# Decay sums of a gated linear attention with high and low parts of 64 tokens stacked on the contraction rows

## The reference

```python
def gla_chunked(q, k, v, log_a):
    """S_t = diag(a_t) S_{t-1} + k_t v_t^T, o_t = q_t S_t."""
    ...
    bc = jnp.cumsum(ac, axis=3)
    ...
        o_inter = jnp.einsum('bhtk,bhkv->bhtv', qi * jnp.exp(bi), state)
        diff = bi[:, :, :, None, :] - bi[:, :, None, :, :]
        decay = jnp.exp(jnp.where(causal[:, :, None], diff, -jnp.inf))
        scores = jnp.einsum('bhtk,bhsk,bhtsk->bhts', qi, ki, decay)
```

## Time and profile before

| | |
|---|---|
| time of the runs shown | 903.37, 903.11, 903.11 us; median 903.11 |
| span of the profiled execution, first to last instruction | 901.3 us |
| PE busy | 893.6 us, 99% of the span |
| DVE busy | 624.8 us, 69% |
| ACT busy | 504.8 us, 56% |
| POOL busy | 79.0 us, 9% |
| granted TensorE clock, mean | 0.999 |

### The profile page before, as it was taken

How to read it: one execution, slowest core, us unless ns; L and a number is a source line. 1 busy time by engine, 2 the same in 40 slices (tenths; PEclk the granted TensorE clock), 3 DMA queues, 4 the chain that set the end, 5 groups by cost and what they waited for, 6 DMA issues and landing times.

```text
span 901.3 us, 12594 instructions
## 1 busy us (share of the span) xinstructions
PE 893.6 (99%) x4946; PEld 761.6 (85%) x4946; DVE 624.8 (69%) x793; ACT 504.8 (56%) x701; POOL 79.0 (9%) x145
## 2 busy tenths in 40 slices
PE   9999999999999999999999999999999999999998
PEld 7888878887889888888889988777888888888887
DVE  5646566765876566666585898998887595666664
ACT  6646655545355444444466878977464564444441
POOL 8603342130010000000000000000000000000000
PEclk9999999999999999999999999999999999999999
DMA  8654333466554655555545764443446376556551
GB/s 274 222 187 152 128 102 121 152 225 220 184 157 156 218 187 186 186 186 187 187 141 186 236 189 139 134 131 112 139 147 209 111 233 191 185 190 201 182 170 47
DMA packets 103380, 155.27 MB, mean 172 GB/s; under 512 B 2650, under 2 KB 70338, under 8 KB 103331
## 3 DMA queue, kind: packets, MB, share of 16 engines
q1 hardware_dynamic: 102416, 151.57, 51.6%
q0 software_dynamic: 864, 2.98, 1.0%
q10 hardware_dynamic: 50, 0.04, 0.0%
HBM read 153.53 MB, written 1.05 MB: 172 GB/s over the span
## 4 chain that ended last, share of the span: by engine, by line
PE 96%; ACT 1%; issue 1%; POOL 0%; DMA 0%; DVE 0%; POOLq 0%; ACTq 0%; DVEq 0%
PE PS L628 19%; PE PS L630 19%; PE PS L629 19%; PE PS L1017 15%; PE PS L1022 8%; PE PS L681 3%; PE PS L687 1%; PE PS L907 1%; PE PS L1153 1%; PE PS L1131 1%; PE PS L1065 1%; PE PS L1189 1%; PE PS L894 0%; PE PS L858 0%; DMA res<-in_x_dram 0%
## 5 line engine op out<-in xcount | busy, mean ns | idle before, releaser
L1937 DVE TENSOR_TENSOR wlo<-raw,whi 128x2048 fp32r<-128x2048 f32 x141 | 324.2, 2301 | 124.0 <-ACT whi L1341 122.3
L1341 ACT CAST whi<-raw 128x2048 fp32r<-128x2048 f32 x141 | 269.2, 1909 | 112.1 <-PE PS L630 109.2
L1017 PE MATMUL PS<-hT,whi 128*128 128x512 f32 x608 | 144.7, 390 | 0.0
L1017 PEld LDWEIGHTS PS<-hT,whi 128*128 128x128 f32 x608 | 113.2, 188 | 23.2 <-issue 0.2
L628 PE MATMUL PS<-whi,hT 128*128 128x512 f32 (+1 forms) x320 | 126.2, 395 | 0.0
L630 PE MATMUL PS<-whi,hT 128*128 128x512 f32 (+1 forms) x320 | 123.1, 385 | 0.0
L629 PE MATMUL PS<-wlo,hT 128*128 128x512 f32 (+1 forms) x320 | 122.9, 384 | 0.0
L628 PE MATMUL PS<-whi,aT_hi 128*128 128x512 f32 x216 | 84.3, 391 | 0.0
L629 PE MATMUL PS<-wlo,aT_hi 128*128 128x512 f32 x216 | 84.3, 390 | 0.0
L630 PE MATMUL PS<-whi,aT_lo 128*128 128x512 f32 x216 | 84.0, 389 | 0.0
L1022 PEld LDWEIGHTS PS<-hT,wlo 128*128 128x128 f32 x608 | 78.0, 191 | 3.0
(11 more groups left out here) (385 smaller groups left out, 1303.5 us busy)
## 6 DMA issues: line engine op xcount, KB each, us to landing
raw<-in_w_in_dram SPq DMA_DIRECT2D x47, 1024.0 KB, 5.1
raw<-in_w_ff_dram SPq DMA_DIRECT2D x32, 1024.0 KB, 5.5
raw<-in_w_gate_dram SPq DMA_DIRECT2D x11, 1024.0 KB, 5.3
raw<-in_w_up_dram SPq DMA_DIRECT2D x11, 1024.0 KB, 5.3
raw<-in_w_down_dram SPq DMA_DIRECT2D x11, 1024.0 KB, 5.0
raw<-in_w_out_dram SPq DMA_DIRECT2D x8, 1024.0 KB, 5.0
raw<-in_w_proj_gla_dram SPq DMA_DIRECT2D x4, 1024.0 KB, 6.6
raw<-in_w_mem_kv_dram SPq DMA_DIRECT2D x4, 1024.0 KB, 5.0
```

The lines of the kernel that those rows point to most:

```text
L1017: pe.matmul(PS[:, bank + c, :], w_hi[:, k, c * P:(c + 1) * P], hT[:, k, :, :].rearrange("p w t -> p (w t)"), start=k == 0, stop=False, ski ...
L1341: act.copy(whi[:, n % RING, :], raw[:, n % RING, :]).then_inc(hi_made, 1)
L1937: dve.tensor_tensor(wlo[:, n % RING, :], raw[:, n % RING, :], whi[:, n % RING, :].bitcast(F32), ALU.subtract).then_inc(lo_made, 1)
```

## The change

The sums are made of 64 tokens at a time. The 128 rows of the contraction hold the rounded part of 64 tokens and their rest together, so that one matmul adds both. For each unit four matmuls of 256 columns (four levels by 64 tokens) stand in place of four of 512. The matrix `decay_r` is folded: its rows repeat after 64. Sums that reach over the middle of the 128 tokens, which are those of the first and the last block only, are no longer complete; `gla_carry` multiplies the half that lacks it by the factor of the other half (`whole`, one column of `E`). The gate's parts are written in halves of 64 partitions, where DVE's rest goes to the partitions that the rounded part leaves. POOL's constants get eight instructions in place of the rounded copy.

```diff
-        a_hi = [w[:, 10:12, :].rearrange("p f t -> p (f t)") for w in (oT_hi, oT_lo)]
-        a_lo = [aT_lo[:, a, :, :].rearrange("p b t -> p (b t)") for a in range(TT)]
+        a_parts = [[oT_hi[:, 10:12, :].rearrange("p f t -> p (f t)"), oT_lo[:, 10:12, :].rearrange("p f t -> p (f t)")],
+                   [aT_lo[:, i, :, :].rearrange("p b t -> p (b t)") for i in range(2)]]
+        HALF = [slice(0, 64), slice(64, 128)]
...
         def gla_carry(engine, u):
 
             h, a = u // 2, u % 2
-            tok = slice(a * P, a * P + P)
-            if a == 0:
-                return engine.tensor_tensor(K7, E[:, 0, :], gkT[:, h, tok], ALU.mult)
-            return engine.tensor_tensor(Q7, E[:, 7, :], gqT[:, h, tok], ALU.mult)
+            x, src, of = (HALF[0], E[:, 0, :], K7) if a == 0 else (HALF[1], E[:, 7, :], Q7)
+            whole = E[:, 7, P - 1:P] if a == 0 else E[:, 7, 63:64]
+            y = HALF[1 - a]
+            other = (gkT if a == 0 else gqT)[:, h, a * P:a * P + P]
+            if u in SHARED_UNITS:
+                engine.tensor_tensor(of[:, y], src[:, y], other[:, y], ALU.mult)
+                return engine.scalar_tensor_tensor(of[:, x], src[:, x], whole, other[:, x], ALU.mult, ALU.mult)
+            engine.tensor_scalar(of[:, x], src[:, x], whole, None, ALU.mult).then_inc(carry, 1)
+            engine.tensor_tensor(of[:, y], src[:, y], other[:, y], ALU.mult)
+            engine.wait_ge(carry, CARRIES.index(u) + 1)
+            return engine.tensor_tensor(of[:, x], of[:, x], other[:, x], ALU.mult)
...
-            step(pool.tensor_copy(decay_r, decay_sum))
+            first, second = decay_sum[:, :, 0:64], decay_sum[:, :, 64:128]
+            for s in range(2):
+                step(pool.tensor_tensor(decay_r[:, s, 0:1, :], first[:, 7:8, :], second[:, 0:1, :], ALU.add))
+                step(pool.tensor_tensor(decay_r[:, s, 1:7, :], first[:, 1:7, :], second[:, 1:7, :], ALU.add))
+                step(pool.tensor_tensor(decay_r[:, s, 8:9, :], first[:, 8:9, :], second[:, 7:8, :], ALU.add))
+                step(pool.tensor_copy(decay_r[:, s, 7:8, :], decay_r[:, s, 8 * s:8 * s + 1, :].bitcast(F32)))
...
                 for c in range(2):
-                    d = decay_r[:, a + 4 * c:a + 4 * c + 4, :]
-                    pe.matmul(PS[:, 6 + c, :], a_hi[a][:, h * P:(h + 1) * P], d, start=True, stop=False)
-                    mm = pe.matmul(PS[:, 6 + c, :], a_lo[a][:, h * P:(h + 1) * P], d, start=False, stop=True)
+                    for s in range(2):
+                        mm = pe.matmul(PS[:, 6 + c, :].rearrange("p (l t) -> p l t", t=P)[:, :, HALF[s]],
+                                       a_parts[a][s][:, h * P:(h + 1) * P], decay_r[:, s, a + 4 * c:a + 4 * c + 4, :],
+                                       start=True, stop=True)
...
                 act.wait_ge(ga_min, a + 1)
-                act.copy(a_hi[a], t).then_inc(ga_hi, 1)
+                for s in range(2):
+                    act.copy(a_parts[a][s][HALF[s], :], t[HALF[s], :]).then_inc(ga_hi, 1)
...
-                dve.wait_ge(ga_hi, a + 1)
-                dve.tensor_tensor(a_lo[a], t, a_hi[a].bitcast(F32), ALU.subtract).then_inc(ga_made, 1)
+                for s in range(2):
+                    dve.wait_ge(ga_hi, 2 * a + s + 1)
+                    dve.tensor_tensor(a_parts[a][s][HALF[1 - s], :], t[HALF[s], :], a_parts[a][s][HALF[s], :].bitcast(F32),
+                                      ALU.subtract).then_inc(ga_made, 1)
```

More of the change, by code:

```diff
@@ L145, in two_block_kernel @@
         SIG_EXP = [f"gout{c}" for c in range(4)] + ["cg0", "cg1"]
-        CONSTS = 1 + 1 + 4 * LEVELS + 1 + 1 + 3 + 1 + 3 * LEVELS + 1
+        CONSTS = 1 + 1 + 4 * LEVELS + 1 + 8 + 3 + 1 + 3 * LEVELS + 1
         PS = ctx.enter_context(nc.psum_tensor("PS", [P, 8, 512], F32))
@@ L216, in two_block_kernel @@
         decay_sum = TMP[:, 0:1152].rearrange("p (l t) -> p l t", t=P)
-        decay_r = aT_hi[:, :, :, :].rearrange("p r a t -> p (r a t)")[:, 0:1152].rearrange("p (l t) -> p l t", t=P)
+        decay_r = aT_hi[:, :, :, :].rearrange("p r a t -> p (r a t)")[:, 0:1152].rearrange("p (s l t) -> p s l t", s=2, t=64)
         mask = TMP[:, 1152:2176].rearrange("p (l t) -> p l t", t=P)
@@ L227, in two_block_kernel @@
         SHARED_UNITS, LOW_LEVELS = (0, 1, 5, 6, 7), 4
+        CARRIES = [u for u in range(2 * GLA_H) if u not in SHARED_UNITS]
         def gla_factor(engine, u, l):
@@ L317, in two_block_kernel @@
             sem(n) for n in ("ga_y", "ga_l", "ga_min", "ga_hi", "ga_made"))
+        carry = sem("carry")
         gf_sum, gf_exp, gf_qk, gf_up, gs_made, gs_masked, gs_ready, gs_x = (
@@ L843, in sb_scores @@
                     pe.wait_ge(drained[unit_of["sbk0"] % 2], unit_of["sbk0"] // 2 + 1)
-                    pe.wait_ge(ga_made, 2)
+                    pe.wait_ge(ga_made, 2 * TT)
                 for b in range(2):
```

## The result

The changed kernel takes 906.35 us (median of 6, 905.68 to 906.60) beside 903.24 us for the kernel before: a ratio of 1.0034, 95% interval 1.0024 to 1.0043. It is slower by 3.1 us, above the range of 900.5 to 904.5 us, and on the side of the rival with the clock. The profiled span is 903.9 us where it was 901.3.

A forecast was written before the change was run, and what follows sets the result against it. PE bounds the kernel, busy 893.6 of 901.3 us. Matmuls -3.05, unit 3 +2.43 and the gate +0.70 sum to +0.08 us, so 903.2 us; range 900.5 to 904.5 us.

The forecast's parts named there:

- the rival with the clock: After PE's 3.3 us wait in unit 3 the clock falls to 1.2 GHz; 905.2 us at 4 us; chance 0.08.
- the rule S/2: On PE behind unit 3's wait: S us at 1.2 GHz cost S/2; slower than 904.9 us from S = 3.6.
- The matmuls: In the sums, four matmuls of 256 columns for four of 512 save PE 0.435 us a unit; seven units 3.05 us.
- The rival of the weight load: The sums' new matmuls go at their weight load's pace, 191 ns, gaining 0.15 us a unit; 905.2 us; chance 0.05.
- Unit 3: POOL's third carry instruction waits behind DVE's split, PE starts the scores at 132.74 us; cost 2.43 us.
- DVE first: In unit 3 DVE's split starts at 130.22 us, 0.02 us ahead of POOL's third instruction.
- the first rival: In unit 3 POOL's third instruction starts ahead of DVE's split; unit 3 costs 0.31 us, total 901.1 us; chance 0.36.
- The gate: Two more ACT roundings ahead of emptying chunk n = 2 delay PE at chunk n = 4; cost 0.70 us.
- The share that I gave to POOL's constants: At the gate, a POOL sum of 64 columns holds DVE's split 0.32 us at most; 0.17 us taken.
- the rival of the lock at the gate: POOL's 384-column sum starts just ahead of DVE's split at 24.42, gate 1.0 us later; 904.2 us; chance 0.09.
- The other units: Unit 4's carry keeps 0.14 us of room, no cost; units 0, 1, 2, 5, 6 and 7 have more room.

The follow-up runs named there:

- e5: Changed kernel with ten unread 128x128 matmuls on PE ahead of unit 3's scores: 904.62 us, ratio 1.0019 to the kernel before.
- e1: Kernel before with only the sums' matmuls changed, four of 256 columns per unit, half the products left out: 899.91 us beside 903.03.
- e8: Changed kernel with unit 3 shared with DVE and the gate's second half moved behind chunk n = 4: 898.88 us, ratio 0.9953.
- e9: Kernel before with unit 3 shared with DVE and the gate's second half behind chunk n = 4: 902.37 us, ratio 0.9993.
- e4: Changed kernel with one added wait, so DVE starts its split only after POOL's carry of unit 3: 902.76 us, ratio 0.9993.
- e3: Kernel before with only POOL's carry of units 2, 3 and 4 in three instructions: 904.01 us, ratio 1.0012.
- e6: Changed kernel with unit 3 among the units shared between POOL and DVE: 900.21 us, ratio 0.9971 to the kernel before.
- e7: Changed kernel with the gate's second half moved behind chunk n = 4 on ACT and DVE: 905.20 us, ratio 1.0021.

## Why the prediction was wrong, point by point

**The step that failed** is the clock. The forecast had PE wait 3.3 us in unit 3 and kept the granted clock at 1.00 behind it, at no cost, since it had stayed there through a wait of 1.4 us. A wait of 1.4 us says nothing about one of 3.3. PE waited 3.55 us, the clock went to 1.2 GHz for some 3.4 us, and 1.62 us went there. e5 shows it: POOL as late as ever, the clock held, 1.7 us back. This was the slower rival, at a chance of 0.08, with the rule S/2 and, for S = 4, 905.2 us. The rule held (3.4/2 = 1.7 us); the chance did not, for no row had a wait of that length at a clock of 1.00. Of the 3.1 us between 903.2 forecast and 906.35 measured the clock is the largest term; the rest are the gate with 0.41, unit 3 with 0.18, unit 4 with 0.23, the later start with 0.14, and 0.5 us that stay open.

**The matmuls** were right: 0.44 us a unit, 3.1 us in e1, 3.5 us with all eight units in e8 against e9. The rival of the weight load (191 ns for each) is refuted by starts 0.12 us apart.

**Unit 3** was right in mechanism and nearly in size: 2.43 us forecast, 2.55 on the timeline, or 2.61 counted from chunk n = 15. Most of the difference is the split itself, 2.45 us in place of 2.29 behind POOL's second product. What I had by 0.02 us, DVE first, was 0.25 us in truth (130.18 and 130.43), because the scaling by a column takes 0.45 us and not 0.24. The select was the wrong row for it. That DVE came first was called rightly, but by luck: the sum's 0.02 us were smaller than its error of 0.2. With the right value the first rival (0.36) had almost no chance left. e4 (the race undone) and e3 (the race not lost) settle it.

**The gate** was right in mechanism and mis-sized: 0.70 us forecast, 1.25 - 0.14 = 1.11 us in the profile. The base of it, two more roundings, was 1.06 us with each at 0.53; they took 0.64 each, four of them 2.58 us where two had taken 1.05. ACT started line 1416 at 33.02 where line 1400 started at 31.33, 1.69 us later: 1.53 are these roundings, 0.15 a later start of the gate. DVE's emptying ends 1.70 us later, at 34.35, and PE starts 0.14 behind its end. Before, 0.59 us lay between that end and PE's start (33.24 less 31.96 and 0.69), so 0.45 of it was room: 1.70 - 0.45 = 1.25 us. The share that I gave to POOL's constants, 0.17, was small in the profiled execution (the split took 2.38 us, 0.09 more) and is 0.8 us in the profile of e6. The forecast placed a short sum ahead of the split; in three of the six profiles it was the one of 384 columns. So the rival of the lock at the gate (0.09) is real, and its chance was too low, though it doesn't explain the profiled execution.

**The other units** cost little: units 4 to 7 gave 1.51 us of 1.74. The 0.23 us that are missing arise at unit 4, where the forecast had 0.14 us of room left and no cost. The scaling's 0.21 us more use that up. POOL's third product ends at 150.40, PE's last matmul of the chunk starts at 150.09, and the scores, due 0.23 us behind it at 150.32, start at 150.46. The weight load waits too:

```profile
150.08 0.32 POOL L253 TENSOR_TENSOR TMP<-TMP,AR 128x64 f32<-128x64 f32 x1
...
PEld PS L923 <- POOL TMP L253: 0.4, 1, 0.4
```

From there to the next chunk PE takes 1.81 us (150.46 to 152.27) in place of 1.70: 0.14 + 0.11 = 0.25 us.

**The sum** with measured terms: 0.14 + 1.11 - 1.31 + 2.61 + 1.62 - 1.51 = +2.66 us, for a span that grew by 2.6 and a median that grew by 3.1. Without the clock it would be +1.0 us, 904.3 us, inside the range that was given.

What stays open: the median grew by some 0.5 us more than the profiled execution's span; the profiled execution was the shortest of the six (905.68). Two of the six, 906.44 and 906.60 us, have a mean clock of 0.996 where the others have 0.998, and e7's profile with 0.996 shows what that means: a longer stretch at the low clock. The two at 906.32 and 906.38 have 0.998, as the profiled one has, so something else is in them; the lock at the gate, as in e6, or a later start would each do it, and no profile tells which.

## What to carry to other kernels

Read the wait that an edit makes and not only the work that it takes away: on a bound engine a wait is paid in full, and a long one is paid again as a lower clock behind it, which ten matmuls that nobody reads avoided in eight executions of ten (e5), and another engine's help in all nine (e6). Where two engines share something that goes to whoever comes first, compute both arrivals after the change; a faster PE can move the competitor ahead (here DVE by 0.37 us), and a single wait on the engine with room puts the order right. Splitting an instruction by partitions saved nothing on ACT or DVE; its columns were paid twice.

## What the runs showed of the hardware

- TensorE at full clock, idle for 3.5 us and working again: 1.2 GHz from about 134 to 137 us in the changed kernel (matmuls of 512 columns started 0.42 us apart in place of 0.23), and from about 131 to 137 us or later in e7. After the idle stretches of 1.4 and 1.5 us in the profile of e4 it stayed at 1.00; in three other executions of e4 and two of e3 the mean clock was 0.998, and where it fell in them is not known. The Trainium skill (TensorE: Matmul & The Clock Gate, section What's actually happening) says that the clock halves after an idle stretch, and the trace agrees.
- POOL: scaling 64 columns by a column took 0.45 us, a product of 64 columns 0.32, one of 128 columns 0.46, and a sum of 384 columns 1.01 us. So the scaling was the dear one of the two with 64 columns; an affine select of 64 columns took 0.24 us. Whether the operand read as a column or the kind of instruction makes the difference, no run separates.
- ACT: a rounding of 64 partitions by 512 columns took 0.62 us, as one of 128 partitions does, and the next instruction started 0.64 us behind it, where it started 0.53 behind the one of 128. On DVE a subtraction of 64 partitions by 512 columns took 0.69 us, and so did one of 128 partitions.
- POOL and DVE: with both reading SBUF, an instruction issued while the other's ran ended only after it, by its own time less some 0.15 us: 2.38 us in place of 0.33 on POOL, 3.07 in place of 2.29 on DVE. The Trainium skill's exclusive lock (SBUF — State Buffer, section Who interferes with whom) is what these rows show.
